# Expert weights split in units of 2048 columns with three buffers in place of halves of 1024 with six

## The reference

```
def swiglu(x, wg, wu, wd):
    return (jax.nn.silu(x @ wg) * (x @ wu)) @ wd
...
def expert_block(args):
    xb, e = args
    return swiglu(xb, w_gate[e], w_up[e], w_down[e])
```

## Time and profile before

| | us |
|---|---|
| median of 3 runs | 1410.26 (1409.53 to 1412.23) |
| profiled execution | 1410.61 |
| its span, first to last instruction | 1409.0 |
| TensorE busy in the span | 1314.0 (93%) |
| VectorE busy | 1053.0 (75%) |
| ScalarE busy | 904.0 (64%) |

### The profile page before, as it was taken

How to read it: one execution, slowest core, us unless ns; L and a number is a source line. 1 busy time by engine, 2 the same in 40 slices (tenths; PEclk the granted TensorE clock), 3 DMA queues, 4 the chain that set the end, 5 groups by cost and what they waited for, 6 DMA issues and landing times.

```text
span 1409.0 us, 21410 instructions
## 1 busy us (share of the span) xinstructions
PE 1314.0 (93%) x7252; PEld 1103.1 (78%) x7252; DVE 1053.0 (75%) x1532; ACT 904.0 (64%) x1337; POOL 73.8 (5%) x75
## 2 busy tenths in 40 slices
PE   5998999988998999839999999999999999999896
PEld 4988999988936677628888888888888788888684
DVE  5776555557413387549989899899898998998796
ACT  5545444444312287438888798788887987887683
POOL 0010000003200000020000000000000000001600
PEclk9999999998998899969999999999999999999999
DMA  8399544454663001649989899899899998998950
GB/s 323 140 385 408 187 180 180 178 196 165 203 203 120 1 1 40 290 160 416 384 334 418 345 378 413 322 416 394 334 415 362 364 415 324 409 396 323 377 195 31
DMA packets 59423, 392.02 MB, mean 278 GB/s; under 512 B 6654, under 2 KB 12930, under 8 KB 20770
## 3 DMA queue, kind: packets, MB, share of 16 engines
q1 hardware_dynamic: 50578, 354.29, 64.2%
q0 software_dynamic: 8784, 36.92, 7.1%
HBM read 367.93 MB, written 27.45 MB: 281 GB/s over the span
## 4 chain that ended last, share of the span: by engine, by line
PE 84%; DVE 7%; issue 3%; ACT 2%; POOL 2%; DMA 2%; POOLq 1%; ACTq 0%; DVEq 0%
PE bank L1669 15%; PE bank L1671 15%; PE bank L1670 15%; PE bank L1346 8%; PE bank L1347 8%; PE bank L1348 8%; PE bank L1455 2%; PE bank L1654 1%; DVE w_lo L1230 1%; PE bank L1474 1%; PE bank L1559 1%; PE bank L1532 1%; DVE rstd L830 1%; ACT w_hi L730 1%; PE bank L1520 1%
## 5 line engine op out<-in xcount | busy, mean ns | idle before, releaser
L1230 DVE TENSOR_TENSOR w_lo<-raw,w_hi 128x1024 fp32r<-128x1024 f32 x528 | 623.4, 1218 | 32.5 <-ACT w_hi L730 14.6
L730 ACT CAST w_hi<-raw 128x1024 fp32r<-128x1024 f32 x528 | 542.7, 1055 | 88.5 <-PE bank L1671 87.4
L1669 PE MATMUL bank<-w_hi,xg_hi 128*128 128x512 f32 x704 | 275.8, 392 | 0.6 <-DVE xg_lo L1236 0.6
L1671 PE MATMUL bank<-w_hi,xg_lo 128*128 128x512 f32 x704 | 275.0, 391 | 0.0
L1670 PE MATMUL bank<-w_lo,xg_hi 128*128 128x512 f32 x704 | 274.7, 390 | 0.0
L871 DVE TENSOR_TENSOR d_lo<-ring,d_hi 128x1024 fp32r<-128x1024 f32 x120 | 146.6, 1223 | 102.6 <-ACT d_hi L572 102.3
L1346 PE MATMUL bank<-hA_hi,d_hi 128*128 128x264 f32 x640 | 188.0, 294 | 20.2 <-DVE hA_lo L861 15.2
L1347 PE MATMUL bank<-hA_lo,d_hi 128*128 128x264 f32 x640 | 185.2, 289 | 0.0
L1348 PE MATMUL bank<-hA_hi,d_lo 128*128 128x264 f32 x640 | 184.9, 289 | 0.0
L572 ACT CAST d_hi<-ring 128x1024 fp32r<-128x1024 f32 x120 | 125.4, 1046 | 59.0 <-PE bank L1348 51.7
L1669 PEld LDWEIGHTS bank<-w_hi,xg_hi 128*128 128x128 f32 x704 | 132.7, 188 | 28.4 <-issue 1.0
(11 more groups left out here) (314 smaller groups left out, 1593.3 us busy)
## 6 DMA issues: line engine op xcount, KB each, us to landing
raw<-in_moe SPq DMA_DIRECT2D x264, 1024.0 KB, 6.6
ring<-in_wd SPq DMA_DIRECT2D x30, 2048.0 KB, 8.4
out_rows<-zeros POOLq DMA_DIRECT2D x1, 6656.0 KB, 62.6
slot_rows<-zeros POOLq DMA_DIRECT2D x1, 6144.0 KB, 44.9
xs<-slot_rows POOLq DMA_DIRECT2D x8, 512.0 KB, 3.6
out_rows<-yrow POOLq DMA_DIRECT2D x8, 512.0 KB, 7.8
arena<-in_cmp_pages POOLq DMA_DIRECT2D x16, 128.0 KB, 2.4
X2v<-in_cmp_pages POOLq DMA_DIRECT2D x16, 128.0 KB, 2.5
```

Source lines behind the costliest of these rows:

```text
L730: nc.scalar.copy(w_hi[:, i % NSPLIT, :], raw[:, u % NRAW, ITEM * (i % 2):ITEM * (i % 2) + ITEM])\
L1230: V.tensor_tensor(w_lo[:, i % NSPLIT, :], raw[:, (i // 2) % NRAW, ITEM * (i % 2):ITEM * (i % 2) + ITEM], w_hi[:, i % NSPLIT, :].bitcast(F3 ...
L1669: T.matmul(out, lhs_hi, hi, start=first, stop=False)
L1671: return T.matmul(out, lhs_lo, hi, start=False, stop=last)
```

## The change

The item is gone. `w_hi` and `w_lo` have three slots of 2048 columns instead of six of 1024, the same bytes. One cast and one split do a whole unit, and TensorE gives a slot back after 12 products instead of six. `AHEAD` is one unit instead of two items, the same columns. All counts of `lo_ready`, `hi_ready` and `item_used` are halved with it. The loads, their order, the products and their order stay. The diff, cut to its core:

```diff
@@ -50,15 +50,14 @@
...
-UNIT, ITEM = 2048, 1024
+UNIT = 2048
...
-ITEMS = 2 * UNITS
-UP_END = {f: 2 * u + 2 for u, (f, kind) in enumerate(USE) if kind == "b"}
-DOWN_END = {f - 2: 2 * u + 2 for u, (f, kind) in enumerate(USE) if kind == "d"}
+UP_END = {f: u + 1 for u, (f, kind) in enumerate(USE) if kind == "b"}
+DOWN_END = {f - 2: u + 1 for u, (f, kind) in enumerate(USE) if kind == "d"}
...
-NSPLIT = 6
-AHEAD = 2
+NSPLIT = 3
+AHEAD = 1
@@ -244,8 +243,8 @@
...
-        w_hi = sb("w_hi", [P, NSPLIT, ITEM], F32R)
-        w_lo = sb("w_lo", [P, NSPLIT, ITEM], F32R)
+        w_hi = sb("w_hi", [P, NSPLIT, UNIT], F32R)
+        w_lo = sb("w_lo", [P, NSPLIT, UNIT], F32R)
...
@@ -721,18 +720,15 @@
...
-            def round_item(t, i):
-
-                u = i // 2
-                if i % 2 == 0:
-                    act.wait_ge(raw_in[u % NRAW], t * (16 * UNITS // NRAW) + 16 * (u // NRAW + 1))
-                act.wait_ge(item_used, t * ITEMS + i + 1)
-                nc.scalar.copy(w_hi[:, i % NSPLIT, :], raw[:, u % NRAW, ITEM * (i % 2):ITEM * (i % 2) + ITEM])\
-                    .then_inc(hi_ready, 1)
+            def round_unit(t, u):
+
+                act.wait_ge(raw_in[u % NRAW], t * (16 * UNITS // NRAW) + 16 * (u // NRAW + 1))
+                act.wait_ge(item_used, t * UNITS + u + 1)
+                nc.scalar.copy(w_hi[:, u % NSPLIT, :], raw[:, u % NRAW, :]).then_inc(hi_ready, 1)
...
-                round_item(0, i)
+                round_unit(0, i)
...
@@ -761,42 +757,38 @@
...
                     act.wait_ge(hmT_done, t * FT + f + 1)
                     if f >= 2:
-                        act.wait_ge(item_used, t * ITEMS + NSPLIT + DOWN_END[f - 2])
+                        act.wait_ge(item_used, t * UNITS + NSPLIT + DOWN_END[f - 2])
                     nc.scalar.copy(hm_hi[:, f % 2, :, :], (T0, T1)[f % 2][:, 0:256].rearrange("p (k n) -> p k n", n=P))\
                         .then_inc(hmT_hi, 1)
                 n = AHEAD
-                for _ in range(2):
-                    round_item(t, n)
-                    n += 1
+                round_unit(t, n)
+                n += 1
                 rows_out(t)
                 for f in range(FT):
-                    for _ in range(2 * (f >= 2) + 4 * (f + 1 < FT)):
-                        round_item(t, n)
+                    for _ in range((f >= 2) + 2 * (f + 1 < FT)):
+                        round_unit(t, n)
                         n += 1
-                    act.wait_ge(item_used, t * ITEMS + NSPLIT + UP_END[f])
+                    act.wait_ge(item_used, t * UNITS + NSPLIT + UP_END[f])
                     nc.scalar.activation(sg[:, f % 2, :], B[f % 2][:, 0:256], ACT.Silu).then_inc(sg_ready, 1)
                     if f:
...
                     if ends and 4 <= f < 7:
                         back_weighted(f - 4)
-                for _ in range(2):
-                    round_item(t, n)
-                    n += 1
+                round_unit(t, n)
+                n += 1
                 if not ends:
                     gathered(t + 1, 0)
                 transposed(FT - 1)
-                round_item(t, n)
+                round_unit(t, n)
                 n += 1
                 if not ends:
                     gathered(t + 1, 1)
-                round_item(t, n)
-                n += 1
                 if not ends:
                     for i in range(AHEAD):
-                        round_item(t + 1, i)
+                        round_unit(t + 1, i)
             gathered(0, 0)
@@ -1224,11 +1216,11 @@
...
-            def rest_item(t, i):
-
-                dve.wait_ge(hi_ready, t * ITEMS + i + 1)
-                V.tensor_tensor(w_lo[:, i % NSPLIT, :], raw[:, (i // 2) % NRAW, ITEM * (i % 2):ITEM * (i % 2) + ITEM],
-                                w_hi[:, i % NSPLIT, :].bitcast(F32), ALU.subtract).then_inc(lo_ready, 1)
+            def rest_unit(t, u):
+
+                dve.wait_ge(hi_ready, t * UNITS + u + 1)
+                V.tensor_tensor(w_lo[:, u % NSPLIT, :], raw[:, u % NRAW, :], w_hi[:, u % NSPLIT, :].bitcast(F32), ALU.subtract)\
+                    .then_inc(lo_ready, 1)
...
@@ -1265,12 +1257,11 @@
...
-                for _ in range(2):
-                    rest_item(t, n)
-                    n += 1
+                rest_unit(t, n)
+                n += 1
...
-                    for _ in range(2 * (f >= 2) + 4 * (f + 1 < FT)):
-                        rest_item(t, n)
+                    for _ in range((f >= 2) + 2 * (f + 1 < FT)):
+                        rest_unit(t, n)
...
@@ -1660,7 +1648,7 @@
...
-                    pe.wait_ge(lo_ready, t * ITEMS + 2 * NRAW + n + 1)
+                    pe.wait_ge(lo_ready, t * UNITS + NRAW + n + 1)
@@ -1672,23 +1660,25 @@
...
+                    slot = item()
...
-                        slot = item()
...
-                                        slice(512 * half, 512 * half + 512), slot, f == 0 and j == 0, f == FT - 1 and j == 1)
-                        i.then_inc(item_used, 1)
+                                        slice(1024 * j + 512 * half, 1024 * j + 512 * half + 512), slot, f == 0 and j == 0,
+                                        f == FT - 1 and j == 1)
+                    i.then_inc(item_used, 1)
...
-                    for q in range(4):
-                        if f == 0 and q % 2 == 0:
-                            pe.wait_ge(xg_lo_ready, 2 * t + q // 2 + 1)
+                    for q in range(2):
+                        if f == 0:
+                            pe.wait_ge(xg_lo_ready, 2 * t + q + 1)
...
-                        for k in (2 * q, 2 * q + 1):
+                        for j in range(4):
+                            k = 4 * q + j
...
-                                        slice(512 * (k % 2), 512 * (k % 2) + 512), slot, k == 0, k == KC - 1)
+                                        slice(512 * j, 512 * j + 512), slot, k == 0, k == KC - 1)
...
```

More of the change, by code:

```diff
@@ L438, in _ @@
                     sp.dma_start(LT[:], late_in).then_inc(params_in, 16)
-            sp.sem_inc(lo_ready, 2 * NRAW)
+            sp.sem_inc(lo_ready, NRAW)
             sp.sem_inc(item_used, NSPLIT)
@@ L449, in _ @@
                 if u >= NRAW:
-                    sp.wait_ge(lo_ready, 2 * u + 2)
+                    sp.wait_ge(lo_ready, u + 1)
                 sp.dma_start(raw[:, u % NRAW, :], moe[0, u]).then_inc(raw_in[u % NRAW], 16)
@@ L456, in _ @@
                 for u in range(UNITS):
-                    sp.wait_ge(lo_ready, t * ITEMS + 2 * u + 2)
+                    sp.wait_ge(lo_ready, t * UNITS + u + 1)
                     sp.dma_start(raw[:, u % NRAW, :], moe[bass.ds(e, 1), u].rearrange("o p n -> (o p) n"))\
@@ L745, in rows_out @@
             def rows_out(t):
-                act.wait_ge(item_used, t * ITEMS + NSPLIT)
+                act.wait_ge(item_used, t * UNITS + NSPLIT)
                 act.wait_ge(yrow_free, t + 1)
@@ L1253, in _ @@
             for i in range(AHEAD):
-                rest_item(0, i)
+                rest_unit(0, i)
             early_and_last()
@@ L1300, in expert_block @@
                     gathered(t + 1, 1)
-                rest_item(t, n)
-                n += 1
                 if not ends:
                     for i in range(AHEAD):
-                        rest_item(t + 1, i)
+                        rest_unit(t + 1, i)
             with dve.Fori(0, last) as t:
```

## The result

The changed kernel takes 1420.74 us (median of 4 runs, 1420.18 to 1421.90) against 1409.89 for the kernel before (4 runs, 1409.36 to 1412.23): ratio 1.0073, interval 1.0059 to 1.0087. It is slower, as forecast, by 10.9 us where 15.7 were worked out. The profiled execution took 1420.18 us, span 1418.6, against 1410.61 and 1409.0: 9.6 us, and these are accounted for here.

The account below looks back on a forecast made before the run. TensorE was taken to set the pace. Terms of 11.2, 0.9, 1.7 and 1.9 us sum to 15.7, taking the profiled 1410.6 to 1426.3, forecast as 1426 us; own range 1422 to 1431, 8 in 10 1419 to 1435.

Parts of the forecast that it names:

- Prices: Per instruction of 2048 columns: 1.92 us for ScalarE's cast, 2.29 us for VectorE's split.
- The boundary: At seven block boundaries TensorE waits for whole units before d9 and d10: 1.6 us each, 11.2 us.
- the 1.88: At a block's end, TensorE's standstill before d9, started at 904.40 in place of 902.52: 1.88 us.
- First block: TensorE waits for the whole unit b0 in the first block: 0.9 us.
- last block's end: TensorE starts d9 and d10 later at the end of the last block, and all that follows waits: +1.9 us.
- The last block's long wait: +1.7 us: In the last block, TensorE's idle 5.20 us before d3 grows by 1.7 us, as the whole unit must be ready.
- VectorE as the bound: VectorE sets the pace, so each of 264 merged pairs gives back 0.07 us: 18.5 us faster, 1392; chance 0.04.
- Stops covered: Block-end stops fall where TensorE would have waited anyway, so no change: 1410 to 1413; chance 0.03.
- Starvation in mid-block: Three slots come back too late for TensorE in mid-block: 0.3 us at each of 88 steps, 1452; chance 0.05.
- The clock at each boundary: TensorE's clock falls after the stop at each of eight block ends, adding 13 us: 1439; chance 0.07.
- the gap of the earlier trace: TensorE's 2.27 us gap ending at 389.62, after which the clock was at 1.00; only longer stops were to lower it.

Follow-up runs that it names:

- delivery alone: Kernel before, with TensorE waiting for both items of a unit before its first product: 1420.46 us, ratio 1.0071.
- the run with one operand from PSUM: Kernel before, splits in steps 1 to 4 of the last block reading PSUM instead of w_hi, as two operations of 512 columns: 1403.92 us.
- the run in pairs: Kernel before, with VectorE waiting for both casts of a unit before its two splits in steps 1 to 4 of the last block: 1404.08 us.
- the run with fewer loads: Both kernels, with weight loads of blocks 2 to 8 bringing only the first 1024 columns: 1408.1 us (before) and 1421.57 us (changed).
- the run with both early, in items: Kernel before, items of d9 taken ahead of the silu of step 10 and those of d10 ahead of hm_hi: 1403.36 us, ratio 0.9947.
- the run with d9 early: Changed kernel, with the unit of d9 cast and split ahead of the silu and hm of step 10: 1425.07 us, ratio 1.0093.
- early in units: Changed kernel, unit of d9 ahead of the silu and hm of step 10, unit of d10 ahead of hm_hi and hm_lo: 1404.35 us.
- early and later in items: Kernel before, with items of d9 and d10 taken early and the last block's weighting moved to steps 5, 5, 6: 1398.49 us.
- the weighting later: Both kernels, weighting of gathered rows in the last block moved from steps 4, 5, 6 to 5, 5, 6: 1408.74 us (before), 1420.9 us (changed).

## Why the prediction was right, and where it was wrong

**Prices:** right within 0.01 us. **The boundary:** right. It was worked out from the gather transposes on: d10 was to start after 9.01 us and started after 8.98, a0 after 11.89 and came after 11.85. Another 0.25 us per boundary lie in the next block's first step, for which I had put 0.05. One row was read wrongly on the way: the two waits of the weight loads at a boundary are 0.5 us each in the earlier trace rows (6.4 us, 12 times), and the 0.27 is what I had worked out from TensorE's starts; the sum used the starts. The mechanism was the forecast one: a unit delivers nothing until all of it is split, and delivery alone costs 1.41 us.

One reading was too narrow. I put the 1.88 on d9. With d9's unit early, d10's chain alone gives a period of 96.05; the two chains end nearly together, and only both early free the 2 us.

**First block, last block's end:** right (0.9 and 0.93; 1.9 and 1.8).

**The failed step** is "The last block's long wait: +1.7 us", with its reason, "The gather hangs on the copies of `yrow` at the end of the block before, so it moves along with everything". The start of the gathers does hang on them and did move. Their duration I took as fixed, without a row for it. It depends on what VectorE runs beside them: beside back-to-back splits of 1024 columns with both operands in SBUF three gathers took 7.1 to 8.0 us; in the changed kernel one took 7.83 beside three long splits in a row, and the last two, when each long split had to wait some 0.42 us for ScalarE's cast, 2.4 to 2.6. With that the wait of 5.2 us and the lower clock behind it, 6.7 us together, went away instead of growing by 1.7. That the splits hold the gathers, and the gathers make the wait, is shown: the run with one operand from PSUM and the run in pairs each brought the gain into the kernel before, by 0.5 and 0.4%, and in the run with fewer loads the issues stayed as long. That the second SBUF operand does it, and not the length, is not shown by itself.

Which instant frees a held gather is a reading, not an experiment. In the kernel before the three end 0.10 to 0.15 us behind `hm_lo`, but in other runs held gathers end with no `hm_lo` near. What all have in common is a split: outside the run with a PSUM operand the traces have 54 gathers of more than 1.2 us in the last block, and each ends 0.73 to 0.88 us behind the end of a split, about what an undisturbed one takes. Why one split's end frees a gather and the ends before it don't stays open; in the run with both early, in items, a gather of 5.97 us ended behind the fifth of six splits without a gap.

**Range.** 1420.7 lies below the forecast's own 1422 to 1431 and inside the 1419 to 1435 for 8 in 10. That is luck: the lower edge was widened for casts cheaper than my bound, and they cost what was forecast, while the term of the last block's wait came out 8.4 us below its forecast. The 1422 was also set too low for its terms: the lower bounds as written (7 x 1.35, and some 0.2 off each of the other three) give about 1424, an estimate.

**Missed:** 0.8 us at d0 of the last block. VectorE computes the last weights there (with which the gathered rows are added back per token), nine small operations of some 2.1 us, and the unit of d0 has no slack for them; TensorE stops for 0.69:

```profile
1314.45 0.67 DVE L1217 TENSOR_TENSOR Gw<-Gw,Gt 128x128 f32<-128x128 f32 x3
1315.05 6.68 DVE L1222 TENSOR_TENSOR w_lo<-raw,w_hi 128x2048 fp32r<-128x2048 f32 x3
...
1317.38 0.50 PE L1657 MATMUL bank<-w_hi,hm_hi 128*128 128x512 f32 x1 [0.69 <-DVE w_lo L1222]
```

**Rivals.** VectorE as the bound: it saved 21 us and the kernel is slower. Stops covered: d9 comes 1.87 us later. Starvation in mid-block: the waits view has none there. The clock at each boundary: it stayed at 1.00 behind all eight stops of 1.6, so this rival did not come true; but with one of 1.9 (the run with d9 early) it did in 4 of 8 places, so the changed kernel is not far from it, and the gap of the earlier trace rows that I set against it was no safe bound. The traces of the other runs show that directly, since the same gap stands in all of them. In 10 of the 14 traces the clock stays at 1.00 behind it, in four it falls; in the run in pairs, for example (TensorE's timeline, then the window behind it):

```profile
388.92 0.37 PE L1438 MATMUL bank<-consts_sb,arena 48*128 48x48 f32 x3 [2.27 <-ACT arena L650]
...
390.00:394.00 4.00, 3.65 (x12) 2.02 (x11) 1.88 (x3) 0.00 (x0) 0.61 (x1) 0.59 0.39 104
```

What the change costs without the accidental gain: 1.0073 over 0.995 (the run with one operand from PSUM, which left part of the work out) is 1.2%, some 17 us, an estimate over two chips; the same order without any wait for gathers (early in units, less early and later in items) differs by 5.9 us, since there most of the boundary's cost is gone.

## What to carry to other kernels

A larger unit between producer and consumer costs nothing in the steady state while the slack is positive, and up to its whole latency wherever the pipeline drains or refills and the work is not taken up ahead: price it there, times the number of such places. Look first at the order in which the producer takes up its work; casting ahead into slots that were free already gained 0.5%, where the larger unit lost 0.7%. And when a transfer or an indirect gather stands on the path, its duration is a row to be explained, not a constant.

## What the runs showed of the hardware

GpSimd issued a gather of 128 rows in 0.86 to 0.94 us beside splits of 512 columns with one operand in PSUM, and in 7.1 to 8.0 beside back-to-back `tensor_tensor` of 1024 columns with both in SBUF. The Trainium skill (SBUF — State Buffer, "Who interferes with whom") says that a VectorE instruction with two SBUF inputs contends with a GpSimd instruction that reads SBUF, and that whichever issues second waits until the first is through. The trace agrees as to who disturbs whom; it shows more than one instruction's wait, though: a gather outlasted six splits in a row, 6.88 us. What in the gather's issue reads SBUF, no row shows.

TensorE's granted clock stayed at 1.00 (2.4 GHz) behind the eight idle times of 1.6 us of the changed kernel, and behind eight of the same length in each of two more runs with its block ends (the weighting later, fewer loads). It fell (0.64 over 4 us, so partly at 1.2 GHz) behind four of eight of 1.9 us in the run with d9 early, and behind one of 2.27 us in the attention part in four of the 14 traces, in code that is the same in all. So the length of such a stop alone does not say whether the clock falls, and one gap that did no harm proves little.
